# Five projections of the first block by seven half-size products per pair of tiles, and three rotating banks for attention's turned tiles

## What is computed

```
xn = modulate(rmsnorm(h, norm1_g[l]), sh1, sc1)
p = xn @ w_in[l]
qk = silu(causal_dwconv(p[..., OFF_Q:OFF_MV], conv_w[l], conv_b[l]))
y_a = gmlp_branch(p[..., OFF_U:OFF_V], p[..., OFF_V:OFF_Q], ...)
y_b = mlstm_branch(q, k, mv, o, i, f, ...)      # ends with h * sigmoid(o)
merged = sigmoid(ga) * y_a + sigmoid(gb) * y_b
h = h + g1 * (merged @ w_out[l])
```

## Time and profile before

| | us |
|---|---|
| median of 3 runs | 3402.62 (3397.97 to 3402.7) |
| the profiled execution | 3402.94, of which the profile's span is 3401.2 |
| PE busy | 3285.2, 97% of the span |
| DVE busy | 1762.2, 52% |
| ACT busy | 498.0, 15% |
| POOL busy | 87.7, 3% |

### The profile page before, as it was taken

The page is one execution under the profiler, slowest core; times in us unless marked ns, Lnnn a source line. Parts: engine busy times, 40 slices in busy tenths (PEclk is TensorE's granted clock), DMA queues, the critical chain, the costliest instruction groups (busy, mean ns, idle before and its releaser), DMA issues.

```text
span 3401.2 us, 33752 instructions
## 1 busy us (share of the span) xinstructions
PE 3285.2 (97%) x13442; PEld 2425.4 (71%) x13442; DVE 1762.2 (52%) x2968; ACT 498.0 (15%) x1020; POOL 87.7 (3%) x102
## 2 busy tenths in 40 slices
PE   6999999999999999999899999999999988999998
PEld 2444445588888888884447888888888744488886
DVE  4116315565337775382646665376644637366643
ACT  2110101100001000013531000010001045210000
POOL 0000000000000000012000000000000030000000
PEclk8989999999999999999999999999999998999998
DMA  5214331222222222223002222222222230122221
GB/s 207 75 60 148 124 136 37 74 87 87 87 87 78 87 87 86 88 88 123 2 14 86 87 87 81 93 87 87 87 90 84 70 118 0 38 87 87 87 79 58
DMA packets 42845, 285.51 MB, mean 84 GB/s; under 512 B 5216, under 2 KB 5216, under 8 KB 11840
## 3 DMA queue, kind: packets, MB, share of 16 engines
q1 hardware_dynamic: 38592, 268.71, 22.3%
q0 software_dynamic: 4096, 14.64, 1.3%
HBM read 279.14 MB, written 2.10 MB: 83 GB/s over the span
## 4 chain that ended last, share of the span: by engine, by line
PE 86%; DVE 5%; ACT 1%; DVEq 1%; issue 1%; DMA 0%; POOL 0%; ACTq 0%
PE ps L783 61%; PE ps L435 14%; PE ps L454 3%; PE ps L987 2%; PE ps L955 1%; PE ps L969 1%; PE ps L719 1%; ACT arena L1248 1%; DVE arena L1897 1%; PE ps L703 1%; PE ps L994 0%; PE ps L926 0%; PE ps L919 0%; DVE arena L1914 0%; DVE arena L1668 0%
## 5 line engine op out<-in xcount | busy, mean ns | idle before, releaser
L783 PE MATMUL ps<-arena 128*128 128x256 f32 x4624 | 1058.5, 379 | 0.1
L783 PEld LDWEIGHTS ps<-arena 128*128 128x128 f32 x4624 | 878.7, 190 | 120.2 <-DVE arena L1585 0.8
L783 PE MATMUL ps<-arena,ring 128*128 128x256 f32 x2384 | 555.7, 379 | 0.0
L783 PEld LDWEIGHTS ps<-arena,ring 128*128 128x128 f32 x2384 | 453.0, 190 | 61.6
L783 PE MATMUL ps<-xn,ring 128*128 128x256 f32 x1888 | 435.8, 381 | 11.3 <-ACT xn L1136 4.0
L783 PEld LDWEIGHTS ps<-xn,ring 128*128 128x128 f32 x1888 | 359.9, 191 | 70.8 <-issue 9.7
L435 PE MATMUL ps<-xn,ring 128*128 128x512 f32 x768 | 335.1, 599 | 0.4 <-DVE arena L1416 0.4
L1565 DVE TENSOR_TENSOR arena<-arena,ps 128x512 f32<-128x512 f32 x138 | 94.8, 687 | 418.2 <-PE ps L783 416.2
L1542 DVE TENSOR_TENSOR arena<-ring 128x512 f32<-128x512 f32 x182 | 122.9, 675 | 351.5 <-PE ps L783 351.2
L435 PEld LDWEIGHTS ps<-xn,ring 128*128 128x128 f32 x768 | 147.3, 192 | 186.6 <-issue 186.6
L783 PE MATMUL ps<-xn,arena 128*128 128x256 f32 x1072 | 257.8, 380 | 0.0
(11 more groups left out here) (290 smaller groups left out, 2334.7 us busy)
## 6 DMA issues: line engine op xcount, KB each, us to landing
ring<-in_w_up_a SPq DMA_DIRECT2D x44, 1024.0 KB, 4.8
ring<-in_w_up_b SPq DMA_DIRECT2D x44, 1024.0 KB, 4.8
ring<-in_w_ff SPq DMA_DIRECT2D x32, 1024.0 KB, 4.7
ring<-in_w_ada SPq DMA_DIRECT2D x24, 1024.0 KB, 5.9
ring<-in_w_down_a SPq DMA_DIRECT2D x16, 1024.0 KB, 4.8
ring<-in_w_down_b SPq DMA_DIRECT2D x16, 1024.0 KB, 4.8
ring<-in_w_in SPq DMA_DIRECT2D x14, 1024.0 KB, 4.8
ring<-in_w_out SPq DMA_DIRECT2D x12, 1024.0 KB, 4.8
```

What stands on the lines that cost most here:

```text
L783: mm = nc.tensor.matmul(out_ap, w, operand(product, quads[i]), start=at not in opened, stop=last_chunk and i == len(quads) - 1, skip_group ...
```

## The change

- `u`, `ga`, `o`, `gb` and `qk` are made by `seven`, 24 pairs of tiles in all (4, 4, 4, 4 and 8). The weights are stored in the order that `seven` wants. They are numbered ahead of `ff1`'s pairs, and `half_of` says which four banks a pair uses (flipped for the first four pairs; the same as before from `ff1` on).
- The weights' sums of these 24 chunks are made by GpSimd: 4 TENSOR_TENSORs of 128x512 each and a drain after the second and third. They wait for the chunk to have landed and for the chunk two before to be used. DVE makes `xn`'s sums once (4 instructions of 128x1024) and takes each pair out of PSUM as in the feed-forward.
- The order on PE is now `v`, `u`, `mix`, `ga`, `o`, `gb`, `qk`, first half of `mv`, the gate rows, second half of `mv`, then all four cells. The two columns of ada lie inside `gb`'s pair 1 and `qk`'s pair 5 (ahead of its products; the pair's product `a`, which shares a bank with the columns, comes after DVE has read them). The mixing base's two matmuls come ahead of `v`.
- The convolution reads the taken tile in SBUF, no longer PSUM. ada's chunks are spread: one behind each pair of `ga`, `o`, `gb` and of `qk`'s first four.
- In attention every turned tile, spread and head sum goes to the next of three banks (4, 5, 7); a turn waits for the read of the one three before it. `weigh` has bank 6 alone and waits for the `mixed` of the pair before.

```diff
-           + [x for c in range(8) for x in (("qk", c), ("ada1", c))]
-           + each("mv", 2) + each("ada2", 1) + each("mv", 2, 2) + each("ada2", 1, 1)
...
+           + [x for c in range(4) for x in (("ga", c), ("ada1", c))]
+           + [x for c in range(4) for x in (("o", c), ("ada1", 4 + c))]
+           + [x for c in range(4) for x in (("gb", c), ("ada2", c))]
+           + [x for c in range(4) for x in (("qk", c), ("ada2", 4 + c))] + each("qk", 4, 4)
+           + each("mv", 4) + each("out1", 4) + each("ff1", 16) + each("ff2", 16))
...
+            for n, (name, layer, c, quads) in enumerate(SEVEN_CHUNKS[:FIRST_PAIRS]):
...
+                pool.wait_ge(sem(f"landed{slot}"), 16 * before + 16)
+                if n > 1:
+                    earlier = SEVEN_CHUNKS[n - 2]
+                    slot, before = chunk(earlier[0], earlier[2], 0, 0, 0)
+                    pool.wait_ge(sem(f"used{slot}"), before + 1)
...
+                nc.gpsimd.tensor_tensor(s1, a21, a22, ALU.add)
+                nc.gpsimd.tensor_tensor(s3, a11, a21, ALU.subtract)
+                pool.drain()
+                nc.gpsimd.tensor_tensor(s2, s1, a11, ALU.subtract)
+                pool.drain()
+                nc.gpsimd.tensor_tensor(s4, a12, s2, ALU.subtract).then_inc(sem("pool_summed"), 1)
...
+            for p in range(8):
+                if p == 5:
+                    seven("qk", 0, p, UP_QUADS, x1_operand, None, "ebdgcaf", ahead=columns_ahead(2))
+                else:
+                    seven("qk", 0, p, UP_QUADS, x1_operand)
+            pe.wait_ge(sem("pair_taken"), FIRST_PAIRS - 1)
+            pe_token_product(pe, "mv", 0, 0)
...
+            for p in range(8):
+                if p == 5:
+                    ada_take(4, 4 * half_of(SEVEN_AT["qk", 0, 5]) + 3, 32, 16)
+                take_first_pair("qk", p)
+                convolve(2 * p, first_tile1)
+                convolve(2 * p + 1, up_w[:, 0, :])
+                if p < 4:
+                    ada_chunk(2, 4 + p)
+                dve.drain()
...
-                        wait(pe, f"copied{4 + u}", TURNS[u] * layer + TURN["turn", n, u])
+                        wait_turn_bank(pe, (layer, "turn", n, u))
...
-                    wait(pe, "mixed", 8 * layer + j - 1)
+                    wait(pe, "mixed", 8 * layer + j)
```

More of the change, by code:

```diff
@@ L200, in turn_uses, with use @@
 def turn_uses():
[L202 to L217, removed]
+    found, reads = {}, {"act": 0, "dve": 0}
+    def use(key, engine):
+        found[key] = (len(found), engine, reads[engine])
+        reads[engine] += 1
+    for layer in range(LAYERS):
+        for n in range(ATT_STEPS + 7):
+            if 0 <= n - 3 < ATT_STEPS:
+                kind, _, i = step(n - 3)
+                for u in ((i % 2,) if kind == "C" else (0, 1)):
+                    use((layer, "turn", n - 3, u), ("act", "dve")[u])
+            if pair_ending(n - 4) is not None:
+                use((layer, "norm", pair_ending(n - 4)), "act")
+            if head_pair(n - 7) is not None:
+                use((layer, "head", head_pair(n - 7)), "dve")
+    return found
 def head_pair(n):
@@ L473, in row_bank @@
             pair = ROW_PAIR[name]
-            return 4 * (SEVEN_AT[pair[0], layer, pair[1]] % 2) + (2 if name == "s1" else 3)
+            return 4 * half_of(SEVEN_AT[pair[0], layer, pair[1]]) + (2 if name == "s1" else 3)
         def act_square(act, q, slot_buf, src, scale=1.0):
@@ L690, in _ @@
                     .then_inc(sem("spread"), 1)
[L691 to L695, removed]
+            pe_token_product(pe, "mv", 1, ST)
             pe.wait_ge(sem("qk_silu"), 16)
@@ L747, in _ @@
             pe_norm(pe, 0, SQUARES["n2", 0] + DT)
[L748 to L777, removed]
-                            summed = True
-                        if ready is not None:
-                            pe.wait_ge(*ready(product, quads[i]))
-                        if at in read:
-                            pe.wait_ge(*read.pop(at))
-                        mm = nc.tensor.matmul(out_ap, w, operand(product, quads[i]), start=at not in opened,
-                                              stop=last_chunk and i == len(quads) - 1, skip_group_check=True)
-                        opened.add(at)
-                        if last_chunk and product == "a" and i == len(quads) - 1:
-                            mm.then_inc(sem("pair_a"), 1)
-                        elif (product, i) == places[-1]:
-                            mm.then_inc(sem(f"used{slot}"), 1)
@@ L1024, in _, with take_first, first_pairs @@
         def _(act):
+            def take_first(number):
+                act.wait_ge(sem("pair_a"), number + 1)
+                wait(act, "pair_taken", number)
+                nc.scalar.activation(gate_of(number)[:, 2, :], ps[:, 4 * half_of(number) + 3, 0:HALF], ACT.Copy)\
+                    .then_inc(sem("first_taken"), 1)
+            def first_pairs(name, places, function, used=None):
+                n = dict(FIRST_PRODUCTS)[name]
+                for p in range(n):
+                    number = SEVEN_AT[name, 0, p]
+                    take_first(number)
+                    act.wait_ge(sem("pair_taken"), number + 1)
+                    if used is not None:
+                        wait(act, used, 2 * p - 2)
+                    made = (gate1[:, 0:2, :].rearrange("p o s -> p (o s)"), up_w[:, 0, :])
+                    for i in range(2):
+                        nc.scalar.activation(places(2 * p + i), made[i], function).then_inc(sem("first_read"), 1)
             act.wait_ge(sem("in_cols"), 16)
```

434 lines of the change are left out of this document (266 added, 168 removed).

## The result

| | median | of runs | span of the profiled execution |
|---|---|---|---|
| before | 3400.30 us | 4 (3397.44 to 3402.70) | 3401.2 us |
| changed | 3353.39 us | 4 (3349.56 to 3355.66) | 3353.9 us |

The ratio is 0.9861, 95% interval 0.9846 to 0.9876: 47 us faster. I had said 3372 and 3356 to 3381, so the kernel is faster than even the range allowed.

What follows compares the result with a forecast made beforehand. PE, busy 97% of the span, was taken as the bound. 3402.9 - 38.6 - 1.4 + 0.9 + 1.2 - 3.0 = 3362.0, plus 10.5 for DVE and GpSimd alternating, gave 3372.5, stated as 3372 us; range 3356 to 3381.

Steps and rivals of the forecast that it cites:

- 24 pairs: In `u`, `ga`, `o`, `gb` and `qk`, seven products cost 12.13 us a pair instead of 13.74: 38.6 us saved.
- Small terms: Four small effects on PE's path: `mv` loads -1.4 us, first `u` pair +0.9, `mix` +1.2, tail 0.
- load gap between the halves of `mv`: PE's 1.37 us wait for a load inside `mv` goes, as its four loads stand together behind `qk`: -1.4 us.
- ACT's reading of the last `v` tile: The first `u` pair waits for this ACT pass and a hand-over: about +0.9 us, bounded by 0 and 2.
- mixing product: `mix` makes 8 tiles in 4 banks behind DVE's take of `u`'s last pair: +1.2 us, bounded by 0 and 3.
- tail's `centre`: After `mv`, `centre` must run while PE makes the cells' first scores; it fits: 0, at worst +3 us.
- Moved at the same price: The gate rows' spread, ada columns and mixing base's matmuls move in the first block, with their slow clock: nothing.
- slow start: PE's slower running: 1 us after the idle stretch in `qk`; behind the moved ada columns, carried over at nothing.
- Alternation of DVE and GpSimd: In `qk` the two engines exclude one another and PE waits: 9.5 us, 10.5 with slower restart; chance 0.50.
- Attention: With three banks, each PE wait for ACT's copies shrinks by 0.5 us at most: -3 us, bounds 0 and 13.
- Rival 1: In `qk` DVE runs its chain through, GpSimd fitting into takes and idle stretches: 3364 us, range 3354 to 3366; chance 0.33.

Runs made afterwards that it cites:

- the first block alone: The changed kernel with the old attention (turns in banks 4 and 5, `weigh` in 6 and 7): 3374.44 us, ratio 0.9921 to the kernel before.
- columns later: The changed kernel with the last ada columns made ahead of `qk` pair 6, not 5, and taken between DVE's two convolutions of pair 5: 3344.36 us.
- and ada chunk first: The changed kernel with the last ada columns one pair later and DVE's ada chunk ahead of the convolutions in `qk`'s first four pairs: 3342.69 us.

## Why the prediction was wrong

**24 pairs: right.** 12.13 us a pair were forecast. `u` took 48.59/4 = 12.15 a pair, and `ga`, `o` and the first `gb` pair 108.78/9 = 12.09.

**Small terms: right or near.** The load gap between the halves of `mv` is gone. `u` waits 1.0 us for ACT's reading of the last `v` tile (forecast 0.9). The mixing product takes 172.41 - 162.79 = 9.6 us instead of 7.8, so +1.8 (forecast +1.2, though the steps written there, 8.8 less 7.8, give 1.0). The tail's `centre` costs 0.2 us (forecast 0).

**Moved at the same price: right for the spread.** The slow start did move: the second half of `mv`, behind the spread, takes 30.10 us, the first 27.47. Behind the first columns it comes in some executions only.

**Alternation of DVE and GpSimd: right in mechanism, in place and in the sum.** I had forecast three stops of PE, 1.3 + 2.0 + 6.2 = 9.5 us. The trace has them in `qk3`, `qk4` and ahead of `qk5`, with 2.7 and 0.3 (for GpSimd) and 6.5 (for DVE's last ada chunk): 9.5. The two smaller ones were each off, so that the sum agrees to the tenth is luck; in the trace of the first block alone it is 3.3 + 5.4 = 8.7. GpSimd's addition was priced at 1.18 us and takes 1.27 to 1.43 in its groups' means from `ga` to `gb`. The timelines of DVE and GpSimd (start, us) at the last of them:

```profile
386.53 4.93 DVE L1623 SCALAR_TENSOR_TENSOR arena<-up_w,cols,arena 128x511 f32<-128x511 f32 x3
391.39 3.35 DVE L1412 SCALAR_TENSOR_TENSOR arena<-ring,stat,arena 128x2048 f32<-128x2048 f32 x1
```

```profile
390.88 1.71 POOL L650 TENSOR_TENSOR arena<-ring 128x512 f32<-128x512 f32 x1
392.73 3.14 POOL L652 TENSOR_TENSOR arena<-arena,ring 128x512 f32<-128x512 f32 x1
```

Three 0.75 us operations take 4.93 us, and a GpSimd addition that came up beside the long ada chunk takes 3.14. What I under-priced is the slow start: 1 us forecast, where the columns alone took 6.96 us and not 3.5, with clock 0.50 over 395 to 402 us. The next pairs were slow as well: in the trace of the first block alone the three pairs behind those columns take 38.80 us, not 36.4. The first block's total is right all the same, 27.4 us forecast and 27.4 measured, and that is luck too. The kernel before lost 1.8 us behind each of its two sets of columns (56.74 against 54.95, 6.12 against 4.31); I had carried both over at nothing, and in that trace `gb` runs on at full clock behind the first set, and the cells' scores take 4.3 to 4.6.

**Attention: this step failed.** I wrote: "each wait shrinks by 0.5 at most", "The bounds are 0 and 2 x 13 x 0.5 = 13 us", and took -3. The chip gives 23.4. This term alone is 20 us off, and it accounts for the whole miss: 3372.5 - 20.4 = 3352. Four faults, each shown above:

1. *The bound was built on one row.* The earlier trace rows is one pair of waits. It fell by 4.3 us in layer 0 and 3.7 in layer 1, 8.0 where I took 3, and inside the bound of 13. But the head sums (3.5 us), the turn behind the spread's copy (0.8) and the normaliser (0.7) wait behind the same two banks. I had put them at nothing, and they are gone from both layers: 10.0 us. Other rows took 4.2 back.
2. *The records were priced as if they kept their length.* PE's own records are 4.4 us shorter in layer 0 and 6.8 in layer 1. I had the clock's effect in mind in the first block and not here. How much of it PE would otherwise have waited is open, as "columns later" shows.
3. *"ACT's queue and not the bank is what makes the copy late" was half right, and the conclusion wrong.* ACT's queue does set when the copy comes. That doesn't make PE wait: with two banks for ACT's uses the row goes from 12.0 us to 0.7.
4. *A wait that two engines pass back and forth was counted once.* At the head sums PE waits for DVE and then DVE for PE, and the reciprocal of 3.35 us starts late.

So the bound of 0.5 us a wait held for the one row and was none for the stage. A gain in one step may also let the next begin from a better place. How much of the gain is such carrying over was not told apart: no run gives every kind of use its own bank, since there are only eight.

Rival 1's far end, "with attention's bound of 13 in full, 3352", is near the measured time, but by another sum: it had no alternation in it.

## What to carry to other kernels

Where engines take turns over a few PSUM banks, let every short-lived use take the next bank of one shared ring rather than own one: three shared banks gave 23.4 us here, the third bank in one or two owners' hands at most 12.5, and a fourth one, with the long-lived use in the ring too, nothing. Price such a change by all waits that stand behind the banks, look at what clock PE has after each, and take the sum of one row of waits neither as a bound nor as a gain, since the second-latest engine is in no list. Where work on GpSimd is to run beside DVE, look for the point at which PE needs the last of DVE's chain, and put that point one stage later.

## What the runs showed of the hardware

- A DVE instruction of 0.75 us with two SBUF inputs takes 1.60 us when GpSimd's additions alternate with it, and its group's mean over `qk` is 1187 ns against 750 without them. GpSimd's addition of 128x512 took 1.26 us at best and 3.14 beside a long DVE instruction.
- After an idle stretch of 6.5 us, 32 records of 128x1 took 6.96 us at a granted clock of 0.50; without the stretch they took 3.46. Behind a stop of 2.5 us, in "and ada chunk first", they took 6.98. After a stop of 2.33 us two records of 128x512 took 2.00 us, not 1.09.
- Whether the clock falls behind the first ada columns differs between executions of the same code (0.57 or 1.00 over 7 us, 3.0 us in `gb`).
